# Five slots for gathered rows and six for units of v in the down stage, instead of four and seven

## The chip, the cores and the metric

One core of one Trainium2 chip runs the program. The metric is the device time of one execution in microseconds (us), the median of several. Three runs of the kernel before gave 1728.82, 1731.11 and 1731.68 us, so its median is 1731.11 us.

## The reference, cut to what matters

One decoder layer on 256 tokens of 2048 channels, float32 in and out. A projection, two convolutions (31 taps and 3 taps), an output projection and a first layer norm give x1. Then comes a block of experts with product keys, and that is where nearly all of the time and of the traffic lies:

```
q = x1 @ w_q ; s = q against sub_keys            # 8 heads, 2 halves, 128 keys
experts = the 16 best of 16 x 16 pairs of keys   # per token and head, out of 16384
g = softmax(top scores)
act[t,h,k] = gelu(x1[t] . peer_u[experts[t,h,k]])
f[t] = sum over h,k of act * g * peer_v[experts[t,h,k]]
out = LN2(2**0.25 * x1 + f)
```

peer_u and peer_v are 16384 x 2048 float32 each, 134 MB each.

## The kernel before, in words

The kernel mostly doesn't gather. It computes the hidden value of every one of the 16384 experts for all 256 tokens (stage **up**, 256 units of u), multiplies each by its gate (zero where the token did not choose the expert), and multiplies the result with the whole of v (stage **down**, 256 units of v). A unit is 128 partitions x 1024 float32, 512 KB. For precision each unit is split in two: ScalarE rounds it to fp32r (`w_hi`, line 641), VectorE subtracts that from the raw unit (`w_lo`, line 861), and TensorE multiplies three products of high and low parts (lines 1638 to 1640). ScalarE runs 4 units ahead of TensorE (`HLEAD`), VectorE 3 (`LEAD`), and the parts have 4 buffers (`SPLIT`), so `hi` of unit u waits until TensorE has used unit u - 4.

**One part of down is gathered.** For the second block of 128 tokens and the first 1024 of the 2048 columns of the output, down does not use TensorE. Each token has 128 picks (8 heads x 16). GpSimd gathers, for pick k, one row of v per token with an indirect DMA (`gather_rows`, line 595: 128 rows of 4 KB, 512 KB per pick, from a copy of v in row order that the up stage writes), and one activation per token (`gather_acts`, line 601, into `sp_coef`). VectorE adds coefficient times row into PSUM (`pick`, line 1340). The 128 picks are spread evenly over units 13 to 239 of the 256 of down: pick k stands at unit `13 + 227*k // 128`, so 128 picks in 227 units.

**The order within down.** Columns are handled in quarters j = 0..3, experts in 32 groups of 4 tiles. A group is 8 units in the order j = 0, 2, 1, 3 with two halves each. Quarters 0 and 1 need TensorE for one block of tokens (6 products of 512 columns a unit), quarters 2 and 3 for two blocks (12 products). In every second group from group 4 to 26 unit number 5 of the group is not split: TensorE multiplies it straight from the raw slot in float32 (`down_unsplit`, line 1649). There are 12 such units. Two groups, 16 units, are one period of this pattern; I call it a double group. At the first unit of a group ScalarE also rounds the coefficients of the next group (`c_hi`, line 794), behind `hi` of the unit 4 ahead, and VectorE subtracts them (`c_lo`, line 1321). The last four groups are walked quarter by quarter.

**The slots.** Raw units lie in a ring. Up to unit 3 of down it has `RAW = 4` slots; from `U_DEEP` on it has `RING = RAW + RAW_LATE` slots, because the space of `xt` (x1 transposed, needed by up alone) is free then: `raw_late` lies there. Rows have `ROWS` slots: `rows` also lie in the space of `xt`, and the last of them (`row_late`) lies in another free place. SyncE issues all loads of units in one queue, in order (`load`, line 482): before unit u it waits until the unit that had the slot, u - RING, has been subtracted by VectorE, or, if that unit is not split, until TensorE has used it. GpSimd issues gathers in order: row k waits until pick k - ROWS is done. A slot of either kind is 4 KB per partition, 512 KB in all.

**The order of GpSimd's gathers.** Row 0, then 8 activation gathers, rows 1 to ROWS - 1, and then for each k from ROWS on: row k, and the activation gathers from `acts_issued(k - 1)` to `acts_issued(k)`. That is two per row for the first eight of these rows and one per row after, until all 128 are issued:

```
def acts_issued(k):
    n = max(0, k - ROWS + 1)
    return min(PICKS, PICKS_IN + min(2 * n, n + PICKS_IN))
```

Every engine works through its list in the order written; nothing is scheduled at run time but by semaphores.

Of the kernel before, what the change touches and what calls it, by code (L numbers as in the profile page):

```python
# [30 lines left out]
JCOLS = JOINED * DCH  # L31
NB = T // BATCH
PICKS = HEADS * TOPK
ROWS = 4
PICKS_IN = 8
PART_OF_TILE = 2

# [79 lines left out]

RAW_LATE = 3  # L120
RING = RAW + RAW_LATE
U_DEEP = U_DOWN + RAW

# [37 lines left out]
# [4 lines that stand above are left out]
# [11 lines left out]
def build(nc, x_t, x_nat, w_in, w_out, w_q, u_w, v_w, params, sub_keys, b_out, ln1_g, ln1_b, ln2_g, ln2_b, out):  # L176
# [11 lines left out]
    with ctx:  # L188
        def sb(name, shape, dt, where=ctx):
            return where.enter_context(nc.sbuf_tensor(name, shape, dt))  # L190

        def sem(name):
            return ctx.enter_context(nc.semaphore(name))
# [9 lines left out]
        def coefs(name, where):  # L203
            return [sb(f"{name}_{part}", [P, GROUP, T], f32r, where) for part in ("hi", "lo")]
# [20 lines left out]
        c_sets += [coefs("c1", down1)]  # L225
        raw_late = sb("raw_late", [P, RAW_LATE, HALF * P], f32, down1)
        rows = [sb(f"rows{i}", [P, JCOLS], f32, down1) for i in range(ROWS - 1)] + [row_late]
        down1.close()
# [218 lines left out]
        v_copied = [sem(f"v_copied{i}") for i in range(2)]  # L447
        rows_in = [sem(f"rows_in{i}") for i in range(ROWS)]
        picked_done = sem("picked_done")
# [110 lines left out]
        def _(pool):  # L560
# [30 lines left out]
            def gather_rows(k):  # L591

                if k >= ROWS:
                    pool.wait_ge(picked_done, k - ROWS + 1)
                nc.gpsimd.indirect_dma_start(  # L595
                    rows[k % ROWS][:, :], None, v_rows,
                    bass.IndirectOffsetOnAxis(sp_idx[:, 1, k:k + 1], 0)).then_inc(rows_in[k % ROWS], 16)
# [1151 lines left out]
```

## Time and profile before

| | |
|---|---|
| median of 3 runs | 1731.11 us (1728.82 to 1731.68) |
| the profiled execution | 1735.24 us, its span 1733.2 us |
| TensorE busy, share of the span | 98% |
| VectorE | 84% |
| ScalarE | 49% |
| GpSimd | 31% |
| HBM read and written | 490.98 MB and 79.69 MB |
| stage down | from about 1180 us to the end |

PE is TensorE's matrix product and PEld its weight load, DVE is VectorE, ACT ScalarE, POOL GpSimd, SP SyncE; a q behind a name is the engine's queue. A line L861 is line 861 of the kernel. "Idle before, releaser" says how long an engine sat idle before an instruction, and what ended that. "issue" means that nothing in the profile explains the wait. For a DMA the profile gives the time from issue to landing.

### The profile page before, as it was taken

The page shows a single profiled execution, that of the slowest core. Times are in us where ns is not written, and L with a number is a line of the kernel's source. Part 1 is how long each engine was busy: PE and PEld are TensorE (multiplying, and loading weights), DVE is VectorE, ACT ScalarE, POOL GpSimd, SP SyncE. Part 2 cuts the span into 40 slices and gives each one's busy share as a digit, 9 for nine tenths or more (in the row PEclk, how much of TensorE's full clock was granted, in tenths as well). Part 3 has the DMA queues.
Part 4 walks back from the last instruction along what each step waited for, and adds up shares of the span by engine and source line. Part 5 has one row for each costly group of instructions (what it writes and reads, how often), then busy time and mean ns, then how long its engine had stood idle before and what let it go on. Part 6 is the DMA issues. An engine that isn't in the chain of part 4 may idle for free.

```text
span 1733.2 us, 27897 instructions
## 1 busy us (share of the span) xinstructions
PE 1698.8 (98%) x10126; PEld 1494.8 (86%) x10126; DVE 1460.2 (84%) x2096; ACT 849.6 (49%) x1072; POOL 530.5 (31%) x342
## 2 busy tenths in 40 slices
PE   9999999899999999999999999999899999999997
PEld 8999988799999888888888888888677887877876
DVE  7999997777968788888888888666889999999997
ACT  5544446344544444444445444445445555555544
POOL 0000000287881000000000000003777777877631
PEclk9999999999999999999999999999999999999999
DMA  7788787777787777777777777898999999999995
GB/s 270 268 277 265 236 257 253 279 238 235 245 251 257 236 242 239 241 236 251 234 243 241 239 241 242 272 376 298 364 376 386 399 400 394 398 395 387 396 405 188
DMA packets 173757, 504.73 MB, mean 291 GB/s; under 512 B 19424, under 2 KB 35936, under 8 KB 172640
## 3 DMA queue, kind: packets, MB, share of 16 engines
q1 hardware_dynamic: 134000, 427.08, 71.9%
q0 software_dynamic: 22528, 67.19, 10.1%
q10 hardware_dynamic: 17136, 9.35, 1.8%
q8 instruction: 41, 0.67, 0.2%
q14 instruction: 52, 0.43, 0.1%
HBM read 490.98 MB, written 79.69 MB: 329 GB/s over the span
## 4 chain that ended last, share of the span: by engine, by line
PE 86%; DVE 4%; POOL 3%; issue 3%; DMA 2%; ACT 1%; DVEq 0%; SPq 0%; POOLq 0%; ACTq 0%
PE psum L1459 22%; PE psum L1460 12%; PE psum L1442 8%; PE psum L1444 8%; PE psum L1443 8%; PE psum L1638 7%; PE psum L1640 7%; PE psum L1639 7%; POOL sp_coef L601 2%; PE psum L1604 2%; PE psum L1462 1%; DVE w_lo L861 1%; PE psum L1508 1%; PE psum L1509 1%; PE psum L1510 1%
## 5 line engine op out<-in xcount | busy, mean ns | idle before, releaser
L641 ACT ACTIVATE w_hi<-raw 128x1024 fp32r<-128x1024 f32 x541 | 572.4, 1060 | 640.2 <-PE psum L1462 180.3
L861 DVE TENSOR_TENSOR w_lo<-raw,w_hi 128x1024 fp32r<-128x1024 f32 x473 | 575.0, 1222 | 136.9 <-ACT w_hi L641 133.9
L1459 PE MATMUL psum<-xt,w_hi 128*128 128x512 f32 x1650 | 583.1, 393 | 0.0
L1460 PE MATMUL psum<-xt,w_lo 128*128 128x256 f32 x1760 | 476.9, 281 | 0.0
L1459 PEld LDWEIGHTS psum<-xt,w_hi 128*128 128x128 f32 x1650 | 309.6, 188 | 63.1 <-issue 0.3
L595 POOL DMA_INDIRECT rows<-v_rows,sp_idx x96 | 133.3, 1389 | 712.0 <-issue 672.4
L1460 PEld LDWEIGHTS psum<-xt,w_lo 128*128 128x128 f32 x1760 | 331.9, 189 | 9.4
L1442 PE MATMUL psum<-xt,w_hi 128*128 128x256 f32 x1184 | 333.7, 282 | 3.8 <-issue 2.4
L1443 PE MATMUL psum<-xt,w_hi 128*128 128x256 f32 x1184 | 331.5, 280 | 0.0
L1444 PE MATMUL psum<-xt,w_lo 128*128 128x256 f32 x1184 | 331.2, 280 | 0.0
L1638 PE MATMUL psum<-w_hi,c_hi 128*128 128x512 f32 x728 | 289.9, 398 | 12.3 <-DVE w_lo L861 12.2
L1640 PE MATMUL psum<-w_hi,c_lo 128*128 128x512 f32 x728 | 283.5, 389 | 0.0
L1639 PE MATMUL psum<-w_lo,c_hi 128*128 128x512 f32 x728 | 283.4, 389 | 0.0
L584 POOL TENSOR_TENSOR w_lo<-raw,w_hi 128x1024 fp32r<-128x1024 f32 x68 | 164.3, 2423 | 363.0 <-ACT w_hi L641 362.8
L1442 PEld LDWEIGHTS psum<-xt,w_hi 128*128 128x128 f32 x1184 | 223.6, 189 | 4.6 <-issue 4.1
L1443 PEld LDWEIGHTS psum<-xt,w_hi 128*128 128x128 f32 x1184 | 223.6, 189 | 0.0
L1444 PEld LDWEIGHTS psum<-xt,w_lo 128*128 128x128 f32 x1184 | 223.5, 189 | 0.0
L601 POOL DMA_INDIRECT sp_coef<-hid_spill,sp_idx x128 | 181.3, 1417 | 54.6 <-issue 45.4
L1638 PEld LDWEIGHTS psum<-w_hi,c_hi 128*128 128x128 f32 x728 | 136.7, 188 | 50.5 <-DVE w_lo L861 17.7
L1639 PEld LDWEIGHTS psum<-w_lo,c_hi 128*128 128x128 f32 x728 | 136.7, 188 | 29.9 <-issue 2.6
L1640 PEld LDWEIGHTS psum<-w_hi,c_lo 128*128 128x128 f32 x728 | 136.6, 188 | 28.9
L641 ACT ACTIVATE w_hi<-raw_late 128x1024 fp32r<-128x1024 f32 x99 | 104.9, 1060 | 105.5 <-PE psum L1640 82.8
(175 smaller groups left out, 1688.0 us busy)
## 6 DMA issues: line engine op xcount, KB each, us to landing
raw<-in_u_w_dram SPq DMA_DIRECT2D x256, 512.0 KB, 4.3
raw<-in_v_w_dram SPq DMA_DIRECT2D x148, 512.0 KB, 8.6
v_rows<-in_v_w_dram SPq DMA_DIRECT2D x128, 512.0 KB, 5.2
raw_late<-in_v_w_dram SPq DMA_DIRECT2D x108, 512.0 KB, 8.4
raw<-in_w_in_dram SPq DMA_DIRECT2D x80, 512.0 KB, 4.4
raw<-in_w_out_dram SPq DMA_DIRECT2D x32, 512.0 KB, 4.6
raw<-in_w_q_dram SPq DMA_DIRECT2D x32, 512.0 KB, 4.2
hid_spill<-hid ACTq DMA_DIRECT2D x7, 1024.0 KB, 14.4
```

The lines of the kernel that those rows point to most:

```text
L584: nc.gpsimd.tensor_tensor(w_lo[s][:, :], raw[:, s, :], w_hi[s][:, :].bitcast(f32), ALU.subtract).then_inc(lo_done[s], SPLIT)
L601: nc.gpsimd.indirect_dma_start(sp_coef[:, k:k + 1], None, hid_dram, bass.IndirectOffsetOnAxis(sp_idx[:, 0, k:k + 1], 0)).then_inc(act_in[k ...
L641: nc.scalar.activation(parts_of(slot_u)[0][:, :], raw_of(slot_u), ACT.Copy)\
L861: tt(lo_w[:, :], raw_of(slot_u), hi_w[:, :].bitcast(f32), ALU.subtract).then_inc(lo_done[slot_u % SPLIT], lo_step(u))
L1442: mm(dst, hi_w[:, sl], xt_hi[:, kk, :], start=st, stop=False)
L1443: mm(dst, hi_w[:, sl], xt_lo[:, kk, :], start=False, stop=False)
L1444: i = mm(dst, lo_w[:, sl], xt_hi[:, kk, :], start=False, stop=en)
L1459: mm(both, hi_w[:, sl], x_both, start=st, stop=False)
L1460: i = mm(both[:, 0:T], lo_w[:, sl], xt_hi[:, kk, :], start=False, stop=False)
L1638: mm(v_bank(j, b), c1, w1, start=st, stop=False)
L1639: mm(v_bank(j, b), c1, w2, start=False, stop=False)
L1640: i = mm(v_bank(j, b), c2, w1, start=False, stop=en)
```

## The change

Two constants change. The rows get a fifth slot, the ring of raw units in down has 4 + 2 = 6 slots instead of 4 + 3 = 7; the sum of both kinds, and so the space, stays the same.

```
-ROWS = 4
+ROWS = 5
-RAW_LATE = 3
+RAW_LATE = 2
```

What follows from them: `RING` is 6 and unit u of down is loaded into the slot of unit u - 6; the semaphores follow. `gather_rows(k)` waits for pick k - 5 instead of k - 4, rows 1 to 4 instead of 1 to 3 are issued right behind the first 8 activation gathers, and `acts_issued` counts from one row later, so that the first pair of activation gathers stands behind row 5 instead of row 4, and so on: each activation gather is issued behind the row after the one it was behind.

## Rows read from the trace of the kernel before

**Rows 1.** The page, part 1: busy us, share of the span, instructions.
```profile
PE 1698.8 (98%) x10126; PEld 1494.8 (86%) x10126; DVE 1460.2 (84%) x2096; ACT 849.6 (49%) x1072; POOL 530.5 (31%) x342
```

**Rows 2.** Busy time by stretch: us, five engines, granted clock, DMA share, GB/s.
```profile
1214.00:1224.00 10.00, 8.36 (x35) 6.61 (x36) 10.00 (x9) 4.41 (x5) 8.37 (x6) 1.00 0.84 274
...
1256.00:1272.00 16.00, 15.64 (x63) 11.66 (x64) 13.48 (x12) 6.09 (x6) 12.81 (x10) 1.00 0.96 338
...
1306.00:1366.00 60.00, 59.79 (x259) 48.21 (x258) 54.63 (x50) 32.07 (x31) 44.74 (x33) 1.00 1.03 399
...
1538.00:1566.00 28.00, 26.73 (x118) 21.84 (x117) 25.59 (x23) 14.30 (x14) 22.52 (x17) 1.00 1.02 400
1566.00:1572.00 6.00, 6.00 (x24) 4.25 (x23) 6.00 (x6) 4.17 (x5) 5.12 (x3) 1.00 0.87 307
```

**Rows 3.** Waits of PE from 1224 to 1283 us: total us, times, longest.
```profile
PE psum L1638 <- DVE w_lo L861: 6.9, 7, 1.7
```

**Rows 4.** Timeline of DVE: start, us, instruction, idle before and releaser.
```profile
1275.45 1.29 DVE L1340 SCALAR_TENSOR_TENSOR psum<-row_late,sp_coef,psum 128x1024 f32<-128x1024 f32 x1 [2.92 <-issue]
...
1548.63 1.29 DVE L1340 SCALAR_TENSOR_TENSOR psum<-rows,sp_coef,psum 128x1024 f32<-128x1024 f32 x1 [1.22 <-DMA rows<-v_rows,sp_idx]
```

**Rows 5.** The chain that ended last: start us, us, what.
```profile
1269.93 8.40 DMA rows<-v_rows,sp_idx
...
1432.29 1.72 PE psum L1649 x4
...
1450.38 0.24 PE psum L1638
...
1465.36 1.72 PE psum L1649 x4
```

**Rows 6.** Waits of SP's queue over the whole span.
```profile
SPq L482 <- PE psum L1649: 42.6, 12, 3.8
```

**Rows 7.** Timeline of POOL at the start of the gathers.
```profile
1219.51 0.94 POOL L595 DMA_INDIRECT rows<-v_rows,sp_idx  x1 [0.30 <-issue]
...
1224.21 1.91 POOL L595 DMA_INDIRECT rows<-v_rows,sp_idx  x1 [0.30 <-DVE psum L1340]
...
1262.80 0.94 POOL L595 DMA_INDIRECT rows<-v_rows,sp_idx  x1 [0.30 <-issue]
...
1265.30 2.00 POOL L595 DMA_INDIRECT row_late<-v_rows,sp_idx  x1 [0.30 <-issue]
```

**Rows 8.** Loads of units (L482) issued between 1306 and 1366 us.
```profile
DMA to landing us min/median/max: 6.4/10.8/12.8
```

**Rows 9.** Gathers of rows (L595) issued between 1290 and 1690 us.
```profile
DMA to landing us min/median/max: 5.3/8.1/10.8
```

**Rows 10.** The first load behind the unsplit unit that ends at 1434.01.
```profile
L482 SPq DMA_DIRECT2D raw<-in_v_w_dram x1: 327/327/327, 1434.0 to 1434.0; - x1
...
DMA to landing us min/median/max: 6.5/6.5/6.5
```

**Rows 11.** The second load there, issued at 1434.4.
```profile
DMA to landing us min/median/max: 8.3/8.3/8.3
```

**Rows 12.** Timeline of ACT behind it.
```profile
1440.95 1.06 ACT L641 ACTIVATE w_hi<-raw 128x1024 fp32r<-128x1024 f32 x1 [0.30 <-PE psum L1640]
1441.92 1.04 ACT L794 ACTIVATE c_hi<-hid 128x1024 fp32r<-128x1024 f32 x1
```

**Rows 13.** Timeline of DVE behind it.
```profile
1443.00 1.22 DVE L1321 TENSOR_TENSOR c_lo<-hid,c_hi 128x1024 fp32r<-128x1024 f32 x1 [1.02 <-ACT c_hi L794]
...
1448.80 1.22 DVE L861 TENSOR_TENSOR w_lo<-raw,w_hi 128x1024 fp32r<-128x1024 f32 x1
```

**Rows 14.** The second load behind the unsplit unit ending near 1568, issued at 1568.5.
```profile
DMA to landing us min/median/max: 5.0/5.0/5.0
```

**Rows 15.** Timeline of ACT at the last unit.
```profile
1706.58 1.06 ACT L641 ACTIVATE tail_hi<-raw_late 128x1024 fp32r<-128x1024 f32 x1 [1.35 <-DMA raw_late<-in_v_w_dram]
```

**Rows 16.** Timeline of DVE at the last two units.
```profile
1708.56 2.34 DVE L861 TENSOR_TENSOR tail_lo<-raw_late,tail_hi 128x1024 fp32r<-128x1024 f32 x2
```

## The prediction, made before the changed kernel was run

> **What bounds the kernel now.** I read the page first, then the stretches of the down stage, then who waits for whom there, then single instructions around the two kinds of slot.
>
> TensorE is busy 98% of the span [rows 1], so only two things can change the time: idle time of TensorE that goes, or new idle time. The reader is to see in the stretches [rows 2] that in down three engines are near their limit together. In 1306 to 1366 TensorE is busy 59.79 of 60 us, VectorE 54.63, and the DMA engines move 399 GB/s. The highest rate in any long stretch with both kinds of gather is 400 to 401 GB/s, which I take as what the DMA engines give here. A double group of 16 units takes 1465.36 - 1432.29 = 33.07 us, from the start of one unsplit unit to the next [rows 5]. It needs 16 units and 16 x 128/227 = 9.02 rows of 0.524 MB, 13.12 MB, or 397 GB/s. So the spare DMA time is 33.07 x (400/397 - 1) = 0.25 us per double group.
>
> Where TensorE idles in down: 6.9 us in 7 waits between 1224 and 1283, all for `w_lo` [rows 3], and 28.00 - 26.73 = 1.3 us between 1538 and 1566 [rows 2]. Both have the same cause one step on. VectorE works in order, and a pick whose row has not landed holds up the subtractions behind it: 2.92 us before the pick at 1275.45, 1.22 us before the one at 1548.63 [rows 4]. The chain of waits runs there through a gather issued at 1269.93 that lands 8.40 us later [rows 5]. So row slots have been short twice. Raw slots have never made TensorE wait in the steady part, but they are what stops SP: 12 times, 42.6 us in all, 3.8 at the longest, it stands before a load until an unsplit unit has been multiplied [rows 6].
>
> **The fifth row slot, early part.** Row k + 1 is issued where row k was in GpSimd's order, since the activation gathers move back by one row too. One place is 1224.21 - 1219.51 = 4.7 us with two activation gathers between, and 1265.30 - 1262.80 = 2.5 us with one [rows 7]. Slots hardly hold this up: GpSimd goes back to back there, with the same 0.30 us of idle time before all four, though at 1224.21 a pick ended no earlier. The gather of 1269.93 would be issued at about 1265.30, 4.6 us sooner. But the bytes must come too. Up to 1283 the DMA engines have room for 16 x (1 - 338/400) = 2.5 us in 1256 to 1272, and for 10 x (1 - 274/400) = 3.2 us in 1214 to 1224 [rows 2]; of the latter the change uses little, for one row more in flight stands against one unit less. The bounds are 0 (the DMA engines take it all back) and 6.9 us (all waits go) [rows 3]. I take 3.5 us gained, between the room of 2.5 and the shift of 4.6. What is late next there is the raw unit.
>
> **The fifth row slot, later.** From 1283 on rows have time: they land 8.1 us after issue at the median [rows 9], a slot comes round every 4 x 33.07/9.02 = 14.7 us, and only the wait of 1548.63 cost anything. With 18.3 us it goes: 1.3 us gained, bounds 0 and 1.3. The activation gathers come one row later, but a batch of eight is issued behind the row of pick 8j - 4 instead of 8j - 5, at least four picks before its use; this costs nothing as long as GpSimd is ahead of VectorE by that much.
>
> **The missing raw slot, between blocks.** A slot comes round every 6 x 33.07/16 = 12.4 us instead of 14.5. Loads take 10.8 us at the median in the deepest stretch [rows 8]. That looks fatal, since 1.06 us of `hi`, 1.22 of `lo` and their waits come on top. But those 10.8 us are mostly queueing behind the kernel's own loads: at 0.524 MB / 400 GB/s = 1.31 us of DMA time a unit, a load issued one unit later finds one unit less ahead of it and lands when it did. So I cost this at nothing while the queue never runs dry. If that cover is gone the price is up to the 2.07 us of a unit.
>
> **The missing raw slot, at a block.** Take the unsplit unit U ending at 1432.29 + 1.72 = 1434.01 [rows 5]. Before, SP stands there before the load of U + 7, issues it at 1434.0, and it lands after 6.5 us [rows 10], at 1440.5. ScalarE takes it at 1440.95, when TensorE frees the buffer, 0.45 us later [rows 12]. Behind that `hi` stand `c_hi` at 1441.92, then on VectorE `c_lo` at 1443.00 and, gapless, the subtractions up to that of U + 9, which starts at 1448.80 and ends at 1450.02 [rows 12, 13]. TensorE starts U + 9 at 1450.38 [rows 5]: 0.36 us of slack. After, SP stands before U + 6, and U + 7 is the second load, 0.4 us later. The second load took 8.3 us [rows 11], which would put U + 7 at 1442.7, 1.8 us behind ScalarE's turn and, less 0.36, 1.4 us of idle TensorE. In the thin state of the queue it took 5.0 [rows 14] and would be in time. Which one holds depends on the queue: with six slots one unit less is in flight when the block lifts, so U + 7 stands where it stood before, and lands near 1440.5 plus at most the 0.4 us. That is inside 0.45 + 0.36.
>
> What is left is DMA time lost while SP is blocked. At 1566 to 1572 the rate fell to 307 GB/s, 6 x (1 - 307/400) = 1.4 us lost in one block [rows 2], more than the 0.25 us spare. With one unit less in flight up to another 1.31 us is lost per block; rows in flight fill part of it. Bounds per block: 0, as in 1306 to 1366 where nothing is lost at 399 GB/s, and 1.31 - 0.25 = 1.06. I take 0.25 us, near the lower end, because falling behind makes the queue deeper and ends the loss: 12 x 0.25 = 3.0 us lost, bounds 0 and 12.7.
>
> The Trainium skill bears on this: "DMA: Bandwidth & Descriptors", section "Queues, rings and completion order", says each DMA engine takes turns between the queues that have work, a packet at a time. The trace agrees, rows landing after 8.1 us where units take 10.8 [rows 8, 9]. By that rule a row issued one pick ahead takes its turns from the units, up to 1.3 us once, not per block, and this speaks against the change at the early part only. The sum without it is the one below.
>
> **The end.** The last loads are issued one subtraction later, about 1.1 us. The `hi` of the last unit waits for its load, from 1.35 us before 1706.58 [rows 15], so it comes 1.1 us later, at 1707.7 to 1708.8. VectorE takes the last two units from 1708.56 on, the last at about 1709.7 [rows 16]. Hidden, with 0.9 us to spare; without it, the 1.1 us would show.
>
> **Sum.** -3.5 - 1.3 + 3.0 = -1.8 us. The profiled execution took 1735.24 us, so 1733.4; it was 4.13 us above the median of the runs, so the median comes to 1731.11 - 1.8 = 1729.3 us.
>
> **The rivals.**
>
> *The rows' gain stands, the raw slot costs nothing.* For it: TensorE idles 0.21 us in 1306 to 1366 while loads take up to 12.8 us [rows 2, 8], so units have slack that no row shows used up. Against it: the spare of 0.25 us. Early part 5.5, later 1.3: 1731.1 - 6.8 = 1724.3 us.
>
> *The block becomes the bound: slower.* The mechanism is the one of U + 7: if its load lands more than 6.94 + 0.36 = 7.3 us after the unsplit unit ends, `c_hi`, `c_lo` and three subtractions come late and TensorE waits. For it: 8.3 us [rows 11], and only 0.45 us in hand before. Against it: the shorter queue. At 1.4 us in 8 of 12 blocks it costs 11.2; less the 4.8 gained, 1731.1 + 6.4 = 1737.5 us. It turns the sign from 0.4 us a block on (4.8 / 12).
>
> *The change doesn't do what it says.* The early rows are late because of GpSimd's own pace, 4.7 us a place against 33.07/9.02 = 3.67 us a pick, and the DMA engines, not for want of a slot. Then nothing moves: 1731 us. Against it: the order shifts by a place whatever the slots do.
>
> **Numbers.** A measurement of this kernel tells 0.2% (3.5 us) from no change. Forecast 0.38: faster 0.10, same 0.25, slower 0.03. Gain stands 0.27: 0.24, 0.03, 0. Block is the bound 0.27: 0, 0.04, 0.23. No effect 0.08: 0, 0.07, 0.01. Together faster 0.34, same 0.39, slower 0.27. The forecast's own range is 1726 to 1733. The whole range must reach both sides: 1723.5, past the case in which the gain stands, to 1738.5, past the block at 1.4 us in 8 of 12.
>
> **What would show it.** Right: the seven waits of TensorE in 1224 to 1283 shrink from 6.9 to about 3 us; no wait for a row near 1548; loads in the deep stretch take 8 to 9 us instead of 10.8 with `hi` still starting on landing; SP's 12 waits for unsplit units stay. Wrong: `hi` of U + 7 late at each block, idle time of VectorE before `c_lo` over 1.5 us instead of 1.02, and TensorE idle once per double group, at U + 9; or the rate in down under 395 GB/s. If the early waits don't shrink, the account of GpSimd's order is wrong.

## The result, and the profile after

The changed kernel takes 1739.26 us (1734.85 to 1743.33, 8 runs), the kernel before 1730.74 (1727.68 to 1734.52, 8 runs): a ratio of 1.0042, 95% interval 1.0029 to 1.0055. It is 8.5 us slower by the medians, 7.3 by the ratio, outside the range that was given, with the sign of the rival "block becomes the bound". Its profiled execution took 1743.33 us (span 1741.3), 4.07 above its median, about as far as that of before (4.13), so the two traces can be set against each other: 8.1 us of span.

The page of the kernel after, part 1, answers to [rows 1]:

```profile
PE 1700.6 (98%) x10126; PEld 1493.8 (86%) x10126; DVE 1461.0 (84%) x2096; ACT 850.2 (49%) x1072; POOL 535.2 (31%) x342
```

TensorE does the same instructions. Of the 8.1 us, 1.8 are busy time and 6.3 idle time: (1741.3 - 1700.6) - (1733.2 - 1698.8). The same stretches as in [rows 2], and one longer one; columns as there:

```profile
1214.00:1224.00 10.00, 7.46 (x32) 5.49 (x31) 10.00 (x9) 4.33 (x5) 8.30 (x6) 1.00 0.97 350
1256.00:1272.00 16.00, 14.43 (x59) 10.63 (x58) 12.94 (x11) 7.76 (x8) 11.87 (x8) 1.00 0.95 350
1306.00:1366.00 60.00, 57.16 (x247) 46.02 (x246) 51.87 (x46) 30.66 (x30) 43.33 (x34) 1.00 1.03 400
1538.00:1566.00 28.00, 27.84 (x122) 22.55 (x121) 26.92 (x25) 15.38 (x16) 24.04 (x14) 1.00 0.96 362
1566.00:1572.00 6.00, 6.00 (x25) 4.30 (x24) 5.27 (x5) 3.67 (x4) 4.74 (x5) 1.00 1.02 396
1500.00:1640.00 140.00, 136.40 (x575) 107.18 (x574) 127.66 (x115) 73.54 (x71) 109.54 (x76) 1.00 1.00 382
```

In 1306 to 1366 TensorE is idle 2.84 us where it was idle 0.21, at the same 400 GB/s. In 1538 to 1566 the loss of 1.3 us is gone. Over 1500 to 1640 the rate is 382 GB/s where before had 392 (138.70 us of TensorE). The waits of TensorE, after, from 1195 to 1290, then in 1224 to 1283 (which answers to [rows 3]), then from 1290 to the end; us in total, times, longest:

```profile
PE psum L1638 <- DVE w_lo L861: 7.1, 8, 1.8
...
PE psum L1638 <- DVE w_lo L861: 4.6, 6, 1.3
...
PE psum L1638 <- DVE w_lo L861: 9.7, 12, 2.0
```

And before, first and last of these three stretches:

```profile
PE psum L1638 <- DVE w_lo L861: 9.2, 9, 1.7
...
PE psum L1638 <- DVE w_lo L861: 3.0, 5, 1.3
```

The early part won 2.1 us of waits, the rest lost 6.7. Counted by units, from the start of one subtraction to that of another: units 17 to 60 of down took 97.5 us before and 94.7 after, 2.8 won. Units 60 to 247 took 386.8 and 396.4, 9.6 lost. I use these two distances below, early and steady; each is from a single profiled execution.

The largest wait of the steady part lies at 1331.5, in front of unit 68, 2.02 us. ScalarE's timeline there, after (idle time before and its releaser in brackets):

```profile
1325.89 1.06 ACT L641 ACTIVATE w_hi<-raw_late 128x1024 fp32r<-128x1024 f32 x1 [2.50 <-DMA raw_late<-in_v_w_dram]
1326.86 1.04 ACT L794 ACTIVATE c_hi<-hid 128x1024 fp32r<-128x1024 f32 x1
```

VectorE's, after:

```profile
1327.93 1.23 DVE L1321 TENSOR_TENSOR c_lo<-hid,c_hi 128x1024 fp32r<-128x1024 f32 x1 [3.21 <-ACT c_hi L794]
...
1330.27 1.22 DVE L861 TENSOR_TENSOR w_lo<-raw_late,w_hi 128x1024 fp32r<-128x1024 f32 x1
```

To be read: a load lands late, `hi` of the unit four ahead (unit 68) waits 2.50 us for it, `c_hi` stands behind that `hi` in ScalarE's order though its own data has long been there, and VectorE stands 3.21 us before `c_lo`. Behind `c_lo` stand a pick and the subtraction of unit 68, which has had its `hi` since 1326.95. That subtraction starts at 1330.27 and ends at 1331.49, when TensorE goes on. `c_hi`, `c_lo` and the pick lie between a late unit and TensorE.

This is no place that the rival named, but about half of the waits lie where it had them, behind the unsplit units. Two lines of TensorE's timeline, after:

```profile
1519.86 0.50 PE L1638 MATMUL psum<-w_hi,c_hi 128*128 128x512 f32 x1 [0.86 <-DVE w_lo L861]
...
1654.98 0.50 PE L1638 MATMUL psum<-w_hi,c_hi 128*128 128x512 f32 x1 [1.53 <-DVE w_lo L861]
```

The first is unit 158, U + 9 of the unsplit unit 149; the second is unit 220, U + 7 of 213. VectorE had stood 1.91 and 1.92 us before `c_lo` there. At 213 it is the `hi` of U + 7 that waits for its load, 1.21 us; at 149 the late loads are those of U + 5 and U + 6. Of the 8.4 us that TensorE waits in units 60 to 223, 4.3 fall at units 68, 84 and 164, four behind the first unit of a group that no unsplit unit shortly precedes, and 4.1 at U + 7 to U + 9 of five unsplit units (149, 165, 181, 197 and 213). At the others nothing is lost: behind the one of [rows 10], `hi` of U + 7 starts at 1442.63, released by TensorE and not by its load. Before, the same units lost 1.5 us, 1.27 of it for a row [rows 4]. How often ScalarE waited, and for what, in 1300 to 1640, before:

```profile
ACT w_hi L641 <- PE psum L1640: 120.4, 101, 3.2
ACT w_hi L641 <- DMA raw<-in_v_w_dram: 20.0, 19, 2.1
ACT w_hi L641 <- DMA raw_late<-in_v_w_dram: 14.3, 16, 2.2
```

And after:

```profile
ACT w_hi L641 <- PE psum L1640: 65.2, 58, 2.1
ACT w_hi L641 <- DMA raw<-in_v_w_dram: 58.4, 51, 2.9
ACT w_hi L641 <- DMA raw_late<-in_v_w_dram: 26.8, 21, 2.5
```

`hi` was released by its load 35 times before and 72 times after. So the change took slack from the raw loads, and what pays for it is what stands behind a late `hi`. The count by itself is no price, as the kernels without activation gathers show below.

### The profile page after: what moved, and what is told of

Read it like the earlier page. It is cut to its first block, busy times and chain, and to the rows that moved or that the text cites. A ratio compares the mean times of both kernels' runs of the same rounds, so it can differ in the third digit from the quotient of the medians.

```text
span 1741.3 us, 27897 instructions
## 1 busy us (share of the span) xinstructions
PE 1700.6 (98%) x10126; PEld 1493.8 (86%) x10126; DVE 1461.0 (84%) x2096; ACT 850.2 (49%) x1072; POOL 535.2 (31%) x342
## 4 chain that ended last, share of the span: by engine, by line
PE 77%; POOL 6%; DMA 5%; DVE 5%; issue 5%; ACT 1%; ACTq 1%; DVEq 0%; SPq 0%; POOLq 0%
PE psum L1459 21%; PE psum L1460 12%; PE psum L1442 8%; PE psum L1443 8%; PE psum L1444 8%; PE psum L1638 4%; PE psum L1640 4%; PE psum L1639 4%; POOL sp_coef L601 3%; DMA raw<-in_v_w_dram 2%; DVE w_lo L861 2%; POOL rows L595 2%; PE psum L1604 2%; PE psum L1462 1%; PE psum L1508 1%
## 5 line engine op out<-in xcount | busy, mean ns | idle before, releaser
L641 ACT ACTIVATE w_hi<-raw 128x1024 fp32r<-128x1024 f32 x562 | 594.6, 1060 | 677.3 <-PE psum L1462 178.5
L861 DVE TENSOR_TENSOR w_lo<-raw,w_hi 128x1024 fp32r<-128x1024 f32 x494 | 601.0, 1223 | 143.8 <-ACT w_hi L641 140.5
L595 POOL DMA_INDIRECT rows<-v_rows,sp_idx x103 | 147.9, 1436 | 716.5 <-issue 679.0
L601 POOL DMA_INDIRECT sp_coef<-hid_spill,sp_idx x128 | 176.8, 1381 | 55.0 <-issue 44.9
L1340 DVE SCALAR_TENSOR_TENSOR psum<-rows,sp_coef,psum 128x1024 f32<-128x1024 f32 x102 | 130.8, 1282 | 6.9 <-issue 3.9
```

Source lines behind the costliest of these rows:

```text
L595: nc.gpsimd.indirect_dma_start(rows[k % ROWS][:, :], None, v_rows, bass.IndirectOffsetOnAxis(sp_idx[:, 1, k:k + 1], 0)).then_inc(rows_in[k ...
L601: nc.gpsimd.indirect_dma_start(sp_coef[:, k:k + 1], None, hid_dram, bass.IndirectOffsetOnAxis(sp_idx[:, 0, k:k + 1], 0)).then_inc(act_in[k ...
L641: nc.scalar.activation(parts_of(slot_u)[0][:, :], raw_of(slot_u), ACT.Copy)\
L861: tt(lo_w[:, :], raw_of(slot_u), hi_w[:, :].bitcast(f32), ALU.subtract).then_inc(lo_done[slot_u % SPLIT], lo_step(u))
```

## The experiments

The theories. **A**: the missing raw slot costs it, through `c_hi` behind a late `hi`. It can have two roots: **A1**, loads land late because the DMA engines are nearly full; **A2**, a slot's own turn (subtraction, issue, transfer, `hi`) is too long for six slots whatever the traffic. **B**: the fifth row in flight takes its bytes from the units, and that costs it. Where 0.2% is the question, a ratio to the kernel before on the same chip is given, with its 95% interval. Medians in us, "early" and "steady" from one profiled execution each; before lay at 1731.68, 1731.84, 1731.52 and 1731.42 in the four batches (23 to 32 runs each).

| kernel | rows / raw slots | median | ratio to before | early | steady |
|---|---|---|---|---|---|
| before | 4 / 7 | 1730.74 | | 97.5 | 386.8 |
| after | 5 / 6 | 1739.26 | 1.0042 | 94.7 | 396.4 |
| r4_u6 | 4 / 6 | 1739.67 | 1.0057 (1.0038 to 1.0076) | 96.9 | 393.0 |
| x1_later | 4 / 7 | 1735.22 | 1.0026 (1.0013 to 1.0038) | 101.7 | 385.7 |
| r5_u7 | 5 / 7 | 1732.92 | 1.0006 (0.9995 to 1.0017) | 99.3 | 385.0 |
| after_cfirst | 5 / 6 | 1732.67 | 1.0007 (0.9990 to 1.0023) | 98.4 | 388.5 |
| before_cfirst | 4 / 7 | 1730.66 | 1.0004 (0.9994 to 1.0014) | 96.3 | 385.2 |
| r5_u7_cfirst | 5 / 7 | 1736.03 | 1.0023 (1.0012 to 1.0034) | 101.9 | 383.8 |
| before_noacts | 4 / 7 | 1727.21 | 0.9972 (0.9961 to 0.9984) | 92.7 | 384.0 |
| after_noacts | 5 / 6 | 1734.74 | 1.0022 (1.0009 to 1.0034) | 96.9 | 391.1 |
| before_halfunits | 4 / 7 | 1724.57 | 0.9958 (0.9943 to 0.9974) | 92.3 | 383.7 |
| after_halfunits | 5 / 6 | 1722.64 | 0.9950 (0.9931 to 0.9970) | 91.0 | 385.4 |
| x1_spread | 4 / 7 | 1736.96 | 1.0027 (1.0009 to 1.0045) | 95.1 | 391.2 |
| r5_u7_spread | 5 / 7 | 1733.53 | 1.0010 (0.9995 to 1.0024) | 93.3 | 392.5 |
| r4_u6_cfirst | 4 / 6 | 1733.19 | 1.0009 (0.9995 to 1.0024) | 98.6 | 384.5 |
| r4_u5 | 4 / 5 | 1754.50 | 1.0142 (1.0120 to 1.0164) | 102.3 | 402.5 |
| r5_u7_x1early | 5 / 7 | 1733.02 | 1.0002 (0.9989 to 1.0015) | 93.5 | 385.8 |

**r4_u6: the missing raw slot alone.**

```diff
-RAW_LATE = 3
+RAW_LATE = 2
```

> Four row slots, six slots for units: the raw slot is taken away and nothing is given. Theory A (the whole loss comes from the missing raw slot: with six slots units land later, the rounding of the coefficients stands behind a late unit on ScalarE, and VectorE and TensorE wait; the fifth row slot gains a little): slower than before by 8 to 13 us, at or above the changed kernel (+8.5), TensorE idle 7 us or more in 1300 to 1690. Theory B (the fifth row slot itself does harm, because rows are fetched earlier and take turns from the units): near the kernel before, within 3 us, and faster than the changed kernel.

Measured: 9.9 us slower by the ratio, 8.0 by the medians. The whole loss is there with four row slots, so A stands and B falls.

**x1_later: room for a fifth row slot, without using it.** There is free space for a fifth row slot beside seven raw slots only under a part of `hid` that the eight pieces of x1, read back for the end, take. So they come later.

```diff
-X1_BACK_AT, PIECE_STEP = 26, 1
+X1_BACK_AT, PIECE_STEP = 48, 1
```

> The kernel before, but the eight loads of x1 (2.1 MB) that stand between the units from unit 26 on stand from unit 48 on. A control for the next kernel. Both theories: within 3 us of before; the waits for rows in 1224 to 1283 may shrink from 6.9 us by up to the 5 us that the 2.1 MB take at 400 GB/s, and the same may come back later as late units.

Measured: 4.5 us slower by the ratio, 3.5 by the medians, a miss, for both theories said within 3. In the trace the place is one stretch, 1272 to 1300, where the pieces now meet the full load stream:

```profile
1272.00:1300.00 28.00, 23.38 (x95) 18.49 (x94) 20.90 (x20) 10.73 (x11) 17.23 (x14) 0.94 1.03 400
```

TensorE is idle 4.62 of 28 us at 400 GB/s, where before it is idle 1.82 at 397; another 1.7 us of this trace are a lower clock (last section). The eight pieces are 2.1 MB, 5.2 us at that rate. Moved out of a stretch with room into one without, they cost about what they weigh; x1_spread, below, shows the same size without the clock.

**r5_u7: a fifth row slot and seven raw slots.**

```diff
-ROWS = 4
+ROWS = 5
...
-X1_BACK_AT, PIECE_STEP = 26, 1
+X1_BACK_AT, PIECE_STEP = 48, 1
...
+        rows += [sb("row_hid", [P, JCOLS], f32, down2)]
...
-                    sp.wait_ge(clo_done, 4)
+                    sp.wait_ge(clo_done, 5)
+                    sp.wait_ge(used, USED0 + U_DOWN + 38)
...
             gather_acts(0, acts_issued(ROWS - 1))
+            pool.wait_ge(clo_done, 1)
```

> Five row slots and seven for units: the fifth row slot lies where the first hidden tiles were, x1 is loaded from unit 48 on as in the control. Theory A: against the control 0 to 4 us faster, none of the changed kernel's waits of TensorE after 1300. Theory B: slower than the control by 4 us or more, with TensorE waits after 1300 as in the changed kernel.

Measured: 1.0006, and against x1_later, its proper partner, 0.20% less (3.5 us by the ratios, 2.3 by the medians). Their intervals overlap, so the gain of the fifth row slot is small and not clear of the noise; a harm of 4 us or more, as B has it, is ruled out. TensorE still waits 5.5 us for `w_lo` behind 1290, 1.7 at the longest, 2.9 of it up to 1312, behind the pieces of x1.

**after_cfirst and before_cfirst: the coefficients ahead of the late unit.** ScalarE rounds `c_hi` before `hi` of the unit four ahead.

```diff
             for u in range(U_DOWN, U_END):
+                if u in coef_at:
+                    coef_hi(coef_at[u])
                 if u + HLEAD < U_END and not unsplit(u + HLEAD):
                     hi(u + HLEAD, u + HLEAD)
-                if u in coef_at:
-                    coef_hi(coef_at[u])
```

> The changed kernel, but at the first unit of a group ScalarE rounds the coefficients before the unit four ahead, not behind it, so that they no longer wait for a unit that has not landed. Theory A: the waits at the fourth and fifth unit of the groups (2.02 us at 1331.5, 0.82 at 1365.7, 1.45 at 1535.2, 1.53 at 1655.0) shrink to under 0.5 us each, and 4 to 7 us of the 8.5 come back. Rival C (units are late by themselves, whoever stands behind them): under 2 us come back, and TensorE waits elsewhere for the same units.

> The kernel before with the rounding of the coefficients ahead of the unit four ahead on ScalarE, as in after_cfirst. If that order matters only where units are late (theory A), seven slots leave little to gain: 0 to 3 us faster than before, and the difference between six and seven slots (with five and four row slots) falls from 8.5 us to under 4. If the order is worth the same 6 us here too, it is an improvement of its own and says nothing about the missing slot.

Measured: after_cfirst 1.0007, so most of the changed kernel's loss comes back: 0.35 points of the ratio (6.1 us), 7.5 us by the medians against before of each batch. before_cfirst moves nothing (1.0004), so the order is no gain of its own with seven slots and this traffic; with `c_hi` first the two kernels lie 0.03 points apart. ScalarE's waits from 1300 to 1640 in after_cfirst:

```profile
ACT w_hi L641 <- DMA raw<-in_v_w_dram: 66.6, 54, 3.8
...
ACT w_hi L641 <- DMA raw_late<-in_v_w_dram: 33.8, 30, 3.3
```

Loads are late even more often (84 times), and TensorE feels it little: it waits 4.3 us for `w_lo` behind 1290, 0.9 at the longest, where the changed kernel has 9.7 and 2.0. VectorE's waits of 1306 to 1500 for `c_hi`, in the kernel before:

```profile
DVE c_lo L1321 <- ACT c_hi L794: 12.6, 12, 2.0
```

And in the changed kernel:

```profile
DVE c_lo L1321 <- ACT c_hi L794: 15.1, 11, 3.2
```

In after_cfirst there is none. The waits were there before the change too and cost TensorE next to nothing (0.21 us at one group), because VectorE was far enough ahead; the missing slot made the longest of them longer, 3.2 us for 2.0. Together with the loss that goes when `c_hi` comes first, that shows the place.

**r4_u6_cfirst: the same with four row slots.** Both edits together.

> Six slots for units, four for rows, and the coefficients rounded first. If the wait of the coefficients behind a late unit is how the missing raw slot reaches TensorE, whatever the rows have, 5 to 8 of the 9.9 us of r4_u6 come back: 1733 to 1737 us against 1731.5 of before. If in after_cfirst the fifth row slot did it, under 3 us come back.

Measured: 1.0009 where r4_u6 had 1.0057: 8.3 of its 9.9 us come back, steady 384.5 for 393.0. TensorE has no wait over 0.15 us in units 60 to 223 of its trace, at neither kind of place, so one chain stood behind both. The fifth row slot plays no part in it.

**r5_u7_cfirst: seven raw slots, five row slots, coefficients first.**

> Five row slots, seven for units, x1 loaded from unit 48 on, and the coefficients rounded first: all that helped, together. 2 to 6 us faster than r5_u7, so 0 to 5 us faster than the kernel before. If late units were the only cost of the order, as theory A has it, nearer 2.

Measured: 1.0023, a miss: r5_u7 was expected to keep or gain. Its steady part is the shortest of all, 383.8, and its early part among the longest, 101.9. TensorE's waits there, 1195 to 1290:

```profile
PE psum L1641 <- DVE w_lo L864: 6.3, 4, 2.9
```

Few and long, and behind two of nearly 3 us (at 1250.6 and 1305.8) the granted clock fell (last section). In front of the first, VectorE had stood 4.73 us for activation gathers. The other executions have no trace, but each has its mean granted clock: seven of the twelve have 0.993 or 0.994 and a median of 1737.52 us, the five from 0.995 up 1733.31. So part of this miss goes with the clock. What makes the early part long here, and not in r5_u7, is open.

**before_noacts and after_noacts: some relief for the DMA engines.** Left out are the activation gathers behind the first eight; the picks use those eight coefficients in turn.

```diff
                 gather_rows(k)
-                gather_acts(acts_issued(k - 1), acts_issued(k))
...
-                if k % PICKS_IN == 0:
-                    pick_coefs(k // PICKS_IN)
-                dve.wait_ge(coef_done, k // PICKS_IN + 1)
+                if k == 0:
+                    pick_coefs(0)
+                dve.wait_ge(coef_done, 1)
```

With them go 15 of VectorE's 16 small products for the coefficients and a part of GpSimd's work, so this relieves more than the DMA engines.

> The kernel before without the activation gathers after the first eight; the picks take the eight coefficients in turn. This leaves out 120 small gathers: the rate of the DMA engines was 408 to 411 GB/s in 1640 to 1688, behind the last of these gathers, and 400 to 401 before, so the spare DMA time per double group goes from 0.25 to about 1.1 us. GpSimd's queue is shorter too, so the early waits for rows go: 5 to 9 us faster than before.

> The changed kernel without the activation gathers after the first eight. Theory A1 (six slots are too few because the DMA engines have almost nothing to spare, so that what is lost at one point is not caught up): within 3 us of before_noacts, instead of 8.5 us slower. Theory A2 (six slots are too few by themselves: a slot comes round in 12.4 us and the way from the issue to the end of the subtraction is longer than that): 6 us or more slower than before_noacts.

Measured: both gain, 0.28% (4.8 us, just under the 5 to 9 expected) and 0.20%, but the difference stays 7.5 us by the medians, 8.7 by the ratios, where A1 as I had put it said 3 at most and A2 6 or more. A miss for A1, on this test. ScalarE's waits of 1300 to 1640 tell more than the time. In before_noacts:

```profile
ACT w_hi L640 <- DMA raw<-in_v_w_dram: 0.8, 2, 0.4
ACT w_hi L640 <- DMA raw_late<-in_v_w_dram: 0.4, 1, 0.4
```

In after_noacts:

```profile
ACT w_hi L640 <- DMA raw<-in_v_w_dram: 48.5, 52, 3.2
ACT w_hi L640 <- DMA raw_late<-in_v_w_dram: 26.2, 24, 2.6
```

With seven slots the late loads nearly vanish, 3 in place of 35; with six 76 remain. So a seventh slot that hardly ever had a late load was still worth 7 to 9 us. Either the relief was too small or A2 is right. The next pair decides.

**before_halfunits and after_halfunits: much relief.** From unit 12 of down on only the first 512 of a unit's 1024 columns are loaded (the rest of the slot keeps what it had); every instruction stays, each load is half as large.

```diff
-                sp.dma_start(raw_of(u), src).then_inc(raw_in[raw_slot(u)], 16)
+                n = DCH if isinstance(u, int) and u >= U_DOWN + 12 else 2 * DCH
+                sp.dma_start(raw_of(u)[:, 0:n], src[:, 0:n]).then_inc(raw_in[raw_slot(u)], 16)
```

> The kernel before, but from unit 12 of down on only the first 512 of a unit's 1024 columns are loaded; the rest of the slot keeps what was there, and all else is done as before. The DMA engines then have 270 GB/s to move instead of 397. The early waits for rows shrink, TensorE idles nowhere after 1300: 4 to 8 us faster than before. The partner of the next kernel.

> The changed kernel with half of each unit loaded from unit 12 of down on. What is left of the 8.5 us when the DMA engines are far from full tells the cause. Theory A1 (late units are queueing at nearly full DMA engines, which six slots can't cover): within 2 us of before_halfunits. Theory A2 (six slots are too few whatever the traffic, because SP issues a unit only when VectorE has done the one six back and stands still before unsplit units): 5 us or more slower than before_halfunits, with TensorE waits after 1300.

Measured: 1724.57 and 1722.64. The loss of 8.5 us is gone, the sign turned (-1.9 us, the intervals overlap). In both no wait of a `hi` in 1300 to 1640 is put down to a load; 26 and 18 waits have no releaser that the trace names, the longest 2.1 and 1.7 us, no longer than those that TensorE ends (2.1 and 2.2). The stretch of 1306 to 1366, before_halfunits:

```profile
1306.00:1366.00 60.00, 60.00 (x259) 48.27 (x258) 56.05 (x51) 32.14 (x31) 49.64 (x35) 1.00 0.82 271
```

after_halfunits:

```profile
1306.00:1366.00 60.00, 59.59 (x254) 47.25 (x254) 55.09 (x50) 31.08 (x31) 49.77 (x34) 1.00 0.82 264
```

At 271 and 264 GB/s six slots do what seven do. A2 had said 5 us or more, A1 within 2. So A1: it is traffic, not the fixed part of a slot's turn. One thing changes beside the traffic, a load of half the size is shorter by itself. Half of the 1.31 us of DMA time a unit is 0.66 us, small beside the 3.21 us that VectorE stood before 1327.93, but no run takes the two apart.

**r4_u5: one raw slot less again.**

```diff
-RAW_LATE = 3
+RAW_LATE = 1
```

> Four row slots and five for units: one slot less again than r4_u6. If units are late by queueing, and what six slots lose per block is lost again and more with five, 15 to 35 us slower than r4_u6, with TensorE waits all along from 1224 on and VectorE idle before the coefficients. If the loss were a matter of single disturbances that happen once or twice in a run, another 5 to 10 us only.

Measured: 1754.50, 1.0142, 14.8 us above r4_u6, just under the 15 expected. The first slot costs 9.9 us by the ratio, the second 14.7. Here the waits of TensorE from 1290 on are many and small:

```profile
PE psum L1638 <- DVE w_lo L861: 13.2, 23, 0.8
PE psum L1638 <- issue: 0.7, 2, 0.4
```

The places are the same as with six slots, and most of the time is now lost behind the unsplit units: 9.2 us of the waits in units 60 to 223 lie at U + 7 to U + 9, behind ten of the eleven unsplit units from 53 on, nine of these sixteen waits between 0.66 and 0.67 us. Whether the late units or the coefficients cause them here isn't separated.

**x1_spread and r5_u7_spread: the pieces of x1 one by one.** They start at unit 48 as in x1_later, but stand 20 units apart, all in the steady part.

```diff
-X1_BACK_AT, PIECE_STEP = 26, 1
+X1_BACK_AT, PIECE_STEP = 48, 20
```

> The kernel before with the eight pieces of x1 loaded one behind every 20th unit from unit 48 to 188 instead of eight in a row from unit 26. If the 4.5 us that x1_later lost are the eight pieces in a row (2.1 MB at once in front of the units), they come back: within 2 us of before. If any piece in the steady part costs its 0.65 us of DMA time, 3 to 5 us slower.

> Five row slots and seven for units as in r5_u7, with x1 in pieces as in x1_spread. Against x1_spread the fifth row slot should give 2 to 4 us, as r5_u7 did against x1_later; against the kernel before 1 to 4 us faster if the pieces cost nothing in this place.

Measured: x1_spread 1.0027, a miss, for I had expected spreading to hide them. It moved the loss: early 6.6 us shorter than in x1_later, steady 5.5 longer, with no fall of the clock in its trace. The pieces cost their own 5.2 us wherever the stream is full. r5_u7_spread is 0.17% below x1_spread: the fifth row slot again some 3 us, with intervals that overlap, and not the 1 to 4 us under before that the first guess held out.

**r5_u7_x1early: five and seven, with the pieces in the gap.** Six pieces from unit 26 on as before, the last two at 48 and 49; the fifth row slot as in r5_u7.

```diff
-X1_BACK_AT, PIECE_STEP = 26, 1
+X1_BACK_AT, X1_REST_AT = 26, 48
...
+                i = n - X1_BACK_AT if n < X1_BACK_AT + 6 else n - X1_REST_AT + 6 if n >= X1_REST_AT else -1
```

> Five row slots and seven for units, as r5_u7, but six of the eight pieces of x1 are loaded from unit 26 on as in the kernel before, and the last two at units 48 and 49 (their place is read by the first unsplit unit until then). x1 loaded in the steady part cost 4.5 us; a quarter of it should cost about 1.2, and the fifth row slot gives 3: 0 to 3 us faster than the kernel before.

Measured: 1.0002, no gain. Its profiled execution had the span 1726.6, early 93.5, 4.0 us under before, which its median doesn't bear out: one trace shows the mechanism, not the size. No kernel of these is clearly faster than the kernel before.

## Why the prediction was wrong, by its steps

- **The early gain** (3.5 us forecast): 2.8 by units 17 to 60, the waits in 1224 to 1283 went from 6.9 [rows 3] to 4.6 us (the forecast said about 3). The wait before the pick of 1275.45 [rows 4] didn't go, it is 3.02 us at 1273.95. Five pairs with and without the slot give 2.2 (after and r4_u6), 2.4, 1.8, 4.0 and 0.2 us early (the last from after_cfirst and r4_u6_cfirst) in single executions, and 0.15, 0.20, 0.17, -0.02 and 0.02 points of the ratio, no pair clear of the noise. Four of the five point the right way; the size, 0 to 3.5 us of the whole time, isn't settled better than that.
- **The later gain** (1.3 us): the wait near 1548 went; 1538 to 1566 lost 0.16 us instead of 1.27 [rows 2]. The number is right, but not because of the fifth slot: r4_u6, with four, has no wait for a row there either (its picks from 1541.67 to 1555.84 follow without idle time), and x1_later, also with four, has TensorE busy 140.00 of the 140 us from 1500 to 1640. The wait was an event of one execution.
- **The missing raw slot between blocks** ("So I cost this at nothing while the queue never runs dry"): this is the step that failed. The slot alone cost 9.9 us (r4_u6), and some 8 of them through the coefficients, which stand behind a late `hi` (r4_u6_cfirst, after_cfirst). The argument held for a queue that is only long: a load issued one unit later does find one unit less ahead. But it has no room for what varies. My reading is that slots come free when VectorE has subtracted, so a stall of VectorE delays the next issues, and at 397 GB/s needed of 400 nothing makes up for it; the seventh slot was the reserve for that. The runs show the two ends of it: 35 loads late with seven slots and 72 with six, and no loss at 264 GB/s (after_halfunits). The feedback through SyncE between them is argued.
- My rows held the warning and I read past it: "`hi` still starting on landing" was the sign I named for *right*, though a `hi` that starts on landing is one with no slack left, and [rows 12, 13] had `c_hi` and `c_lo` behind it with 1.02 us of idle time.
- **The missing raw slot at a block** (3.0 us, bounds 0 to 12.7): TensorE lost 4.1 us at U + 7 to U + 9 in the changed kernel and 2.7 in r4_u6, so the size held. The reason given didn't: I had `hi` of U + 7 in time at every block and priced DMA time lost while SP stands. At five of eleven blocks the subtractions came late, and with the coefficients first they cost nothing (r4_u6_cfirst). That the number fits is luck. DMA time lost at blocks isn't separated; r4_u6_cfirst leaves 1.6 us (-0.9 to 4.2) for all that isn't the coefficients.
- **The cover**: "if that cover is gone the price is up to the 2.07 us of a unit". The largest wait was 2.02, in front of one unit. I gave it no count, and the wait is made of `c_hi`, `c_lo` and a pick behind a late load, so the likeness of the two numbers confirms nothing.
- **The rival "block becomes the bound"** (1737.5) had the sign, almost the size and the chain (late `hi`, `c_hi`, `c_lo`, subtractions), and half of the places. Its signs came true in part: `hi` of U + 7 was released by its load at four of the twelve blocks and not at each, idle time of VectorE before `c_lo` over 1.5 us at two blocks (1.91 and 1.92), TensorE idle at U + 9 at five, 0.16 to 0.86 us and 2.2 in all, where it had 1.4 us at eight. The other half of the loss is at the first units of groups with no block before them, which it didn't name. Its sign "rate in down under 395 GB/s" says little: 382 in 1500 to 1640, but the kernel before had 392 there. Whether loads took 8 to 9 us can't be read: the trace of after has no landing times for units.
- **The end**: hidden as forecast. From the subtraction of unit 247 to the last instruction the trace has 35.2 us before and 35.2 after.
- **The rule on turns between queues** ("DMA: Bandwidth & Descriptors" of the Trainium skill, section "Queues, rings and completion order"), by which, as the prediction worked it out, a row more in flight would take from the units: no run here shows a harm by rows. r5_u7 against x1_later and after against r4_u6 both come out below their partners. The landing times of 8.1 and 10.8 us, which the prediction took for agreement with the rule, fit it but don't show it, for up to seven units and four rows are in flight.

What stays open: the exact worth of the fifth row slot, why r5_u7_x1early gains nothing, and why the early part of r5_u7_cfirst is longer than that of r5_u7. Eight raw slots weren't tried.

## What to carry to other kernels

At nearly full DMA engines (397 GB/s needed, 400 given) a slot of a load ring is not priced by the mean latency, nor by how often consumers already start on landing: most of the 141 waits of `hi` in 1300 to 1640 were ended by something else, 35 by a load in the kernel before and 3 in before_noacts, and a slot less cost 7 to 10 us both times. Take a slot away and measure. Look for work that needs no load but stands behind one in an engine's order, and put it ahead: here that alone bought back 6 to 8 us of a loss of 7 to 10. Traffic moved into a full stretch costs its own transfer time, spread or not (5.2 us of bytes, 4.5 to 4.7 us of time).

## What the runs showed of the hardware that was not expected

TensorE's granted clock fell within down, in a kernel in which it is busy 98% of the span. In x1_later, behind a wait of 3.99 us, PE's timeline has the first matmul at 1296.73 with 0.80 us where 0.50 stood at 1289.73:

```profile
1289.73 0.50 PE L1638 MATMUL psum<-w_hi,c_hi 128*128 128x512 f32 x1 [0.64 <-DVE w_lo L861]
...
1296.73 0.80 PE L1638 MATMUL psum<-w_hi,c_hi 128*128 128x512 f32 x1 [3.99 <-DVE w_lo L861]
```

The clock is at 1.2 GHz in place of 2.4 there, and back within the stretch: its mean over 1272 to 1300 is the 0.94 of the row shown above. Seven other kernels had such a fall. The largest is in after_noacts, behind a wait of 2.87 us:

```profile
1224.00:1256.00 32.00, 28.79 (x112) 22.69 (x111) 23.80 (x21) 14.61 (x14) 11.82 (x7) 0.89 1.03 406
```

Waits of 2.02 us in the changed kernel and 2.20 in r4_u6 were followed by no fall, while one of 2.20 in after_cfirst and one of 1.85 in r5_u7_spread were. What is lost beside the wait itself is the stretch times what its mean lacks of 1: 28 x 0.06 = 1.7 us and 32 x 0.11 = 3.5 us. Kernels that differ in where one wait falls can differ by that: the six executions of x1_later with a mean granted clock of 0.993 or 0.994 have a median of 1736.84 us, the six from 0.995 up 1734.16. It is no part of the changed kernel's loss: its trace has no such fall between the start of down and its last microseconds, and its eight executions have a mean granted clock of 0.995, as the kernel before has in the four batches (0.995 to 0.996).
